# Four of eight cache pieces move from the head of the first tail into the second mixer

## The chip, the cores and the metric

The kernel runs on one core of one Trainium2 chip. The metric is the device time of one launch in microseconds (us), lower is better. A profiled execution of the same program gives the trace; times inside the kernel are counted from the start of its span.

## The reference

Two consecutive layers of a decoder trunk, for 256 prompt tokens and 8 samples of 4 tokens each, all in 32-bit floats. Each layer is a mixer (the second one is dilated sliding-window attention over cached keys and values) followed by a tail. In the tail every token picks its experts by a product-key search and reads one row of `u_tab` and one of `v_tab` for each; this is most of the traffic.

```python
def _tail(x, p, norm_ffn, peer_wq, peer_keys, peer_u, peer_v, norm_ple, ple_gate, ple_proj):
    x = x + _peer(_rmsnorm(x, norm_ffn), peer_wq, peer_keys, peer_u, peer_v).astype(x.dtype)
    gate = jax.nn.sigmoid((_rmsnorm(x, norm_ple) @ ple_gate).astype(jnp.float32))
    ...
def _mixer_dilated_sample(h, pos, caches, w_in, w_out):
    ...
        kv_all = jnp.concatenate([cache, kv_new], axis=1)
        o, l = _dilated_gather_attn(q[:, :, gi], kv_all, L, dil, win // dil)
        outs.append(o)
        lses.append(l)
        keep = min(win, L + T)
        bufs.append(kv_all[:, L + T - keep:])
```

The last line matters here: the key and value caches come back as outputs, so their old rows have to be copied from an input tensor to an output tensor. That copy depends on nothing that is computed.

## The kernel before

**Stages.** The program runs in this order: first norm, first mixer (up to about 239 us), first tail (239 to about 1061 us), second mixer (1061 to about 1503 us), second tail (to the end). They are separated by barriers of all engines.

**A tail.** The engines first do a head: the output projection (line 1818), a norm, the query products (1855), the scores, and on DVE the search that yields the indices of the experts. Then come 288 slots of work. For each, POOL issues an indirect DMA (line 2044) that gathers 128 rows of 8 KB, one for each partition, into one of ten ring buffers (six in `tail_ring`, four in `mid_wring`); DVE takes the dot products (line 1621), ACT makes a diagonal matrix from them (1734 to 1742), and PE adds the weighted rows up (1895). A buffer is reused when PE is done with it. The search for the next 32 slots runs on DVE between the dot products of these.

**The cache copies.** They are HBM to HBM transfers that SP issues. The large ones are cut by `roll_pieces` into pieces of 256 rows, 2.1 MB each (written `32x16384` in the order of instructions, `out_kv_s<-in_cache_kv_w` in the trace). The first mixer copies 32 pieces of the three caches. Of the 32 pieces of the largest cache, which are four for each sample, the first mixer copies the first 8, the head of the first tail copies 8 more (line 2003), and the last `4 * LATE` = 16 are left to the second mixer (line 2679). The second tail copies none; its head is otherwise the same.

**SP's order.** SP issues in program order, and all its DMAs go to one hardware queue, q1 in the trace; those that POOL issues go to q0. In the head of the first tail SP issues the tail's weights and constants (lines 1990 to 2001), then the copies (2003), and after a wait for the projections the rest (2005 and 2009).

**The second mixer.** PE goes through 18 weight chunks of 2 MB (`w_qkv`), numbered c = 0 to 17, in a buffer for two. When chunk c has been multiplied, SP issues the load of chunk c + 2 (line 2687), and right behind it `BESIDE[c]` cache pieces (line 2679), before the stores of the sample rows. Beside the products PE works on side jobs: for chunks 3 to 5 and 12 to 14 the cached keys of the samples, for chunks 6 to 8 and 15 to 17 their values. Keys and values reach it through `mix_ring`, four buffers that POOL fills (line 2710), each when PE has freed it.

**How the pieces are dealt out.** `HEAD[0]` is the number that the first tail's head copies, `LATE` the number of samples that are left to the second mixer, and `BESIDE` says behind which chunk how many go. What `BESIDE` does not name, one piece, is issued before chunk 0. Before, the chunks with pieces are 0, 1, 2, 9, 10, 11 and 17.

Of the kernel before, what the change touches and what calls it, by code (L numbers as in the profile page):

```python
# [2056 lines left out]
UNITS = [(j, it) for it in range(2) for j in range(HH)]  # L2057


LATE = 4  # L2060
HEAD = (8, 0)
EARLY = 0
BESIDE = {0: 2, 1: 2, 2: 2, 9: 2, 10: 2, 11: 2, 17: 3}


def late_pieces(T):

    return roll_pieces(T, 2, range(DEC_B - LATE, DEC_B), 256)


def dilated_phase(nc, K, T, wring, w_in, mixT, w_out_in, late_out):
# [16 lines left out]
    with ExitStack() as ctx:  # L2088
# [60 lines left out]
        with nc.Block() as block:  # L2149
# [487 lines left out]
            def _(sp):  # L2637

                def store(n):
                    c, t = JOBS[n]  # L2640
                    half, kind, g = SECTION(c)
                    o, p = TILES[t]
                    heads = slice(half * HH, half * HH + HH)
                    keep = min(PATTERNS[g][0], SEQ)
                    if kind == 0:
                        return
                    if kind == 1:
                        m = TURNED.index(n)
                        sp.wait_ge(roped, m + 1)
                        src, done = rows[:, m % 4], row_stored[m % 4]  # L2650
                    else:
                        sp.wait_ge(copied, n + 1)
                        src, done = (v[:, t, g] if t < 2 else v_rows[:, g:g + 1]), v_stored
                    if t < 2:
                        if kept(g, t):
                            sp.dma_start(T[f"out_kv{g}_p"][0, 0, o - SEQ + keep:o - SEQ + keep + 128, kind - 1, heads, :],
                                         src).then_inc(done, 16)
                        return
                    full = T[f"out_kv{g}_s"].shape[2]
                    for j in range(HH):  # L2660
                        sp.dma_start(T[f"out_kv{g}_s"][0, :, full - DEC_T:full, kind - 1, half * HH + j, :],
                                     src[32 * j:32 * j + 32, 0, :]).then_inc(done, 16)
                    if kind == 2:
                        if half and g == 0:
                            sp.wait_ge(s_out, 1)
                        for j in range(HH):
                            sp.dma_start(v_new[32 * g:32 * g + 32, j * 128:j * 128 + 128], v_rows[32 * j:32 * j + 32, g, :]
                                         ).then_inc(v_moved, 16)
# [7 lines left out]
                def copies(n):  # L2676
                    for _ in range(n):
                        to, frm = late.pop(0)
                        sp.dma_start(to, frm).then_inc(late_out, 16)

                copies(len(late) - sum(BESIDE.values()))
                for c in range(18):
# [7 lines left out]
                    if c == 17:  # L2690
                        store(3 * c + 2)
                    copies(BESIDE.get(c, 0))
                    if c < 17:
# [28 lines left out]
def build(nc, T):  # L2722

    with ExitStack() as ctx:
# [6 lines left out]

        rolls = [(to, frm, cache_out) for gi, samples, rows in ((1, range(DEC_B), 256), (2, range(DEC_B - LATE), 256),
                                                                (0, range(DEC_B), 128))
                 for to, frm in roll_pieces(T, gi, samples, rows)]
        rolls += [(to, frm, cache_out) for to, frm in late_pieces(T)[:EARLY]]
        with ExitStack() as c2:
            P1 = Phase(nc, c2, "mid")
            wring = P1.sb("wring", [128, 2, KC, 512])
            with ExitStack() as c3:
# [3 lines left out]
                first_norm_phase(nc, K, T, hT, [(wpiece[:, s], T["w_ab"][:, s], w_ab_in[s]) for s in range(4)])  # L2743
                conv_delta_phase(nc, K, T, wring, w_ab_in, w_out_in, mixT, rolls[:24] + rolls[24 + HEAD[0]:])
            w_in, w_out1_in = [P1.sem(f"w_in{i}") for i in range(2)], [P1.sem(f"w_out1_in{i}") for i in range(2)]
            tail_phase(nc, K, T, 0, wring, [(wring[:, c], T["w_qkv"][:, c], w_in[c]) for c in range(2)], w_out_in,
                       rolls[24:24 + HEAD[0]])
            dilated_phase(nc, K, T, wring, w_in, mixT, w_out1_in, late_out)
# [8 lines left out]
def roll_pieces(T, gi, samples, rows):  # L2757

    src, dst = T[f"cache_kv_w{PATTERNS[gi][0]}"][0], T[f"out_kv{gi}_s"][0]
    keep = dst.shape[1] - DEC_T  # L2760
    drop = src.shape[1] - keep
    flat = lambda ap: ap.rearrange("r k h e -> r (k h e)")
    return [(flat(dst[b, r:min(r + rows, keep)]), flat(src[b, drop + r:drop + min(r + rows, keep)]))
            for b in samples for r in range(0, keep, rows)]
# [72 lines left out]
```

## Time and profile before

| | us |
|---|---|
| device time, median of 3 runs | 2307.76 |
| lowest and highest | 2306.37, 2308.43 |
| the profiled execution's device time | 2298.09 |
| its span | 2296.3 |
| busy: PE, DVE, ACT, POOL | 1915.7, 1250.6, 768.8, 701.6 |
| DMA queues q0 and q1, data | 669.72 MB, 203.51 MB |
| mean granted clock of TensorE | 0.946 of full speed |

How to read the rows below. In the page, "GB/s" has one number for each fortieth of the span (57.4 us). A row by windows gives, for a stretch of time, its length, the busy time of PE, weight load, DVE, ACT and POOL with the number of instructions, and then the granted TensorE clock, the DMA share and the GB/s. The DMA share is the time that packets took on the 16 DMA engines, over the stretch; packets are booked whole, so short stretches can read a little over 1. A row of the DMA queues gives packets, MB and share. A row by time gives start, duration, engine, line, operation, tiles, count, and in brackets how long the engine had idled before and what released it. SPq is SP's issuing of a DMA. A copy's bytes are counted once.

### The profile page before, as it was taken

What the parts mean: (1) busy time and instruction counts of PE and PEld (TensorE: products, weight loads), DVE (VectorE), ACT (ScalarE), POOL (GpSimd) and SP (SyncE); (2) the same over time, 40 slices, a digit from 0 to 9 for tenths busy, and PEclk for the clock granted to TensorE, in tenths of its full rate; (3) what the DMA queues carried; (4) which work ended last, traced back from release to release, by engine and by line L of the source; (5) the groups of instructions that cost most, each with busy time, mean ns of one, the idle gap of its engine ahead of it and who ended that gap; (6) DMA issues with size and microseconds to landing.
All of it is one profiled execution on the core that took longest, in us unless ns stands there. A gap on an engine that the chain in (4) does not pass through costs nothing. (4 is left out here: it accounts for less than half of the span.)

```text
span 2296.3 us, 25833 instructions
## 1 busy us (share of the span) xinstructions
PE 1915.7 (83%) x9121; PEld 905.4 (39%) x9121; DVE 1250.6 (54%) x3091; ACT 768.8 (33%) x2251; POOL 701.6 (31%) x709
## 2 busy tenths in 40 slices
PE   7997758878889888767999999889897789888865
PEld 6675424432234322223445644554343223332221
DVE  6974346665675777552110301247755766766654
ACT  2322124433443444342110311215433434433443
POOL 3211124434444533430001010014443344444441
PEclk9998879989999999977999999999998999999977
DMA  9999999999999999997979687949999999999995
GB/s 343 397 348 350 326 369 427 426 428 427 427 427 427 405 427 427 427 428 281 363 296 358 250 328 274 344 190 412 427 427 428 427 427 426 427 427 427 426 427 217
DMA packets 120352, 874.87 MB, mean 381 GB/s; under 512 B 19710, under 2 KB 24830, under 8 KB 34456
## 3 DMA queue, kind: packets, MB, share of 16 engines
q0 software_dynamic: 93328, 669.72, 70.2%
q1 hardware_dynamic: 26896, 203.51, 23.8%
q8 instruction: 72, 1.18, 0.2%
q14 instruction: 56, 0.46, 0.1%
HBM read 861.87 MB, written 118.81 MB: 427 GB/s over the span
## 5 line engine op out<-in xcount | busy, mean ns | idle before, releaser
L1895 PE MATMUL tail_acc<-tail_ring,tail_diag 128*128 128x512 f32 x1248 | 622.6, 628 | 154.8 <-ACT tail_diag L1742 153.5
L1621 DVE CUSTOM_DVE_ANT_0 tail_ring<-tail_ring,all_h 128x1024 f32<-128x1024 f32 x348 | 424.2, 1224 | 293.4 <-DMA tail_ring<-in_peer_uv,tail_idx 291.9
L2044 POOL DMA_INDIRECT tail_ring<-in_peer_uv,tail_idx x348 | 366.9, 1054 | 674.5 <-PE tail_acc L1895 487.7
L1895 PE MATMUL tail_acc<-mid_wring,tail_diag 128*128 128x512 f32 x800 | 391.1, 620 | 72.9 <-ACT tail_diag L1742 72.7
L1895 PEld LDWEIGHTS tail_acc<-tail_ring,tail_diag 128*128 128x128 f32 x1248 | 222.3, 194 | 529.7 <-ACT tail_diag L1742 331.7
L1621 DVE CUSTOM_DVE_ANT_0 mid_wring<-mid_wring,all_h 128x1024 f32<-128x1024 f32 x228 | 278.5, 1224 | 174.3 <-DMA mid_wring<-in_peer_uv,tail_idx 173.6
L1734 ACT ACTIVATE tail_gelus<-tail_dots 128x1 f32<-128x1 f32 x576 | 116.4, 202 | 755.6 <-DVE tail_dots L1621 754.8
L2044 POOL DMA_INDIRECT mid_wring<-in_peer_uv,tail_idx x228 | 250.0, 1097 | 315.4 <-PE tail_acc L1895 264.1
L2166 PE MATMUL mix_acc<-mid_wring,all_hT 128*128 128x512 f32 x576 | 273.8, 610 | 1.5 <-PEq L80 1.4
L1895 PEld LDWEIGHTS tail_acc<-mid_wring,tail_diag 128*128 128x128 f32 x800 | 143.1, 193 | 304.8 <-ACT tail_diag L1742 185.1
L1742 ACT ACTIVATE tail_diag<-all_ident,tail_weights 128x128 f32<-128x128 f32 x512 | 205.5, 401 | 24.2 <-PE tail_acc L1895 7.7
L1739 ACT ACTIVATE tail_weights<-tail_gelus,tail_gate 128x1 f32<-128x1 f32 x576 | 169.8, 295 | 18.7
L2166 PEld LDWEIGHTS mix_acc<-mid_wring,all_hT 128*128 128x128 f32 x576 | 103.3, 193 | 111.7 <-issue 111.1
L2390 DVE TENSOR_TENSOR mix_r<-mix_acc,mix_rope 128x128 f32<-128x128 f32 x24 | 7.0, 292 | 190.1 <-ACT mix_rows L2500 190.1
L420 PE MATMUL mix_banks<-all_hT,mid_wring 128*128 128x288 f32 x384 | 104.3, 423 | 3.7 <-DVEq L1012 2.1
L420 PEld LDWEIGHTS mix_banks<-all_hT,mid_wring 128*128 128x128 f32 x384 | 72.4, 195 | 27.3 <-issue 6.1
L2710 POOL DMA_DIRECT2D mix_ring<-in_kT x32 | 17.0, 534 | 215.0 <-PE mix_wide L2207 178.1
L2417 DVE SCALAR_TENSOR_TENSOR mix_s<-mix_scores_p,mix_band 128x384 f32<-128x384 f32 (+1 forms) x12 | 9.1, 755 | 121.0 <-PE mix_scores_p L2281 120.9
L1818 PE MATMUL tail_acc<-mid_wring,all_mixT 128*128 128x512 f32 x128 | 60.7, 633 | 16.2 <-PEq L80 16.2
L1855 PEld LDWEIGHTS tail_spare<-all_hT,tail_w_big 128*128 128x128 f32 x512 | 67.1, 191 | 15.5 <-issue 15.2
L1855 PE MATMUL tail_spare<-all_hT,tail_w_big 128*128 128x128 f32 (+1 forms) x512 | 68.6, 288 | 2.1 <-ACT all_hT L1707 2.1
L1000 DVE SCALAR_TENSOR_TENSOR all_mixT<-mix_padded_a,mix_taps_a,all_mixT 128x256 f32<-128x256 f32 x120 | 62.3, 548 | 1.2
(472 smaller groups left out, 1755.3 us busy)
## 6 DMA issues: line engine op xcount, KB each, us to landing
mid_wring<-in_w_qkv SPq DMA_DIRECT2D x18, 2048.0 KB, 9.5
mix_ring<-in_kT POOLq DMA_DIRECT2D x16, 1024.0 KB, 10.3
mix_ring<-in_v_rows POOLq DMA_DIRECT2D x16, 1024.0 KB, 10.0
out_kv_s<-in_cache_kv_w SPq DMA_DIRECT2D x8, 2016.0 KB
mid_wring<-in_w_ab SPq DMA_DIRECT2D x12, 1024.0 KB, 11.0
mix_ring<-in_kT POOLq DMA_DIRECT2D x16, 768.0 KB, 10.3
mix_ring<-in_v_rows POOLq DMA_DIRECT2D x16, 768.0 KB, 9.6
tail_w_big<-in_w_query SPq DMA_DIRECT2D x8, 1024.0 KB, 9.3
```

What stands on the lines that cost most here:

```text
L420: last = mm(acc_of(j), wpiece[:, s % 4, k, j % 2 * 128:j % 2 * 128 + 128], hT[:, k, :], start=(k == 0), stop=(k == KC - 1))
L1000: ch.step(STT(out=ca[:, c, 0:SEQ], in0=pa[:, c, k:k + SEQ], scalar=wa[:, c, k:k + 1], in1=ca[:, c, 0:SEQ], op0=ALU.mult, op1=ALU.add))
L1621: V.tensor_tensor_reduce(out=u, in0=u, in1=h[:, g, :], scale=1.0, scalar=0.0, op0=ALU.mult, op1=ALU.add, accum_out=dots[:, n:n + 1]).then_ ...
L1734: ch(A(gelus[:, n:n + 1], dots[:, n:n + 1], ACT.Gelu))
L1739: ch(A(weights[:, n:n + 1], gelus[:, n:n + 1], ACT.Copy, scale=gate[:, j, i:i + 1]))
L1742: A(diag[:, n % DIAGS, 0:w], idn[:, 0:w], ACT.Copy, scale=weights[:, n:n + 1]).then_inc(diag_ready, 1)
L1818: last = mm(acc[g][:, c * 512:(c + 1) * 512], mixT[:, k, g * 128:g * 128 + 128], wring[:, c, k, :], start=(k == 0), stop=(k == KC - 1))
L1855: last = mm(sp2[:, i % 2 * 512:i % 2 * 512 + hi - lo], w_query[:, n, k, :], hT[:, k, lo:hi], start=(k == 0), stop=(k == KC - 1))
L1895: last = mm(acc[g][:, c * 512:(c + 1) * 512], diag[:, n % DIAGS, :], v[:, c * 512:(c + 1) * 512], start=first, stop=final)
L2044: pool.indirect_dma_start(slot(r), None, table, bass.IndirectOffsetOnAxis(ap=idx[:, j, i:i + 1], axis=0)).then_inc(landed[r], 16)
L2166: last = mm(acc_of(n), hT[:, kc, o:o + p], w[:, kc, :], start=(kc == 0), stop=(kc == KC - 1))
L2710: pool.dma_start(ring[:, sl % SLOTS_AHEAD, 0:hi - lo], T[name][half, b, :, lo:hi]).then_inc(landed[sl % SLOTS_AHEAD], 16)
```

## The change

Four of the eight pieces that SP issued at line 2003 go to line 2679: one behind the load that follows chunk 5, one behind that of chunk 6, two behind that of chunk 14. `LATE` = 5 hands the four pieces of one more sample to the second mixer, which now has 20. Nothing else is changed; PE, DVE, ACT and POOL have the same instructions in the same order.

```diff
-LATE = 4
-HEAD = (8, 0)
+LATE = 5
+HEAD = (4, 0)
 EARLY = 0
-BESIDE = {0: 2, 1: 2, 2: 2, 9: 2, 10: 2, 11: 2, 17: 3}
+BESIDE = {0: 2, 1: 2, 2: 2, 5: 1, 6: 1, 9: 2, 10: 2, 11: 2, 14: 2, 17: 3}
```

SP's instructions in the head of the first tail, before (-) and now (+). The first two rows load constants, and the last two are the embedding weights and the sample rows:

```order
 L2000 DMA tail0_gain_b<-in_norm_ple 128x1024
 L2001 DMA tail0_pT<-in_pT0 128x576
-L2003 DMA out_kv2_s<-in_cache_kv_w2048 32x16384 x8
+L2003 DMA out_kv2_s<-in_cache_kv_w2048 32x16384 x4
 L2005 DMA all_mixT<-in_w_emb0 128x2048
 L2009 DMA all_h<-all_hs 32x256 x16
```

Four issues are gone between the constants and the embedding weights.

SP's instructions in the second mixer after chunks 5 and 6 of the first half; `mid_wring<-in_w_qkv` is the load of a weight chunk, `mix1_rows`, `mix1_v` and `all_h` are stored as new cache rows, and `mix1_v_new` is filled for the samples' values:

```order
 L2656 DMA out_kv2_p<-mix1_rows 128x512 x2
 L2687 DMA mid_wring<-in_w_qkv 128x4096
+L2679 DMA out_kv2_s<-in_cache_kv_w2048 32x16384
 L2661 DMA out_kv2_s<-mix1_rows 8x4x128 x4
 L2656 DMA out_kv0_p<-mix1_v 128x512
 L2687 DMA mid_wring<-in_w_qkv 128x4096
+L2679 DMA out_kv2_s<-in_cache_kv_w2048 32x16384
 L2661 DMA out_kv0_s<-all_h 8x4x128 x4
 L2667 DMA mix1_v_new<-all_h 32x128 x4
```

A piece stands behind the weight load of chunk 7 and one behind that of chunk 8, ahead of the small stores.

The same engine after chunk 14, in the second half:

```order
 L2656 DMA out_kv2_p<-mix1_rows 128x512 x2
 L2687 DMA mid_wring<-in_w_qkv 128x4096
+L2679 DMA out_kv2_s<-in_cache_kv_w2048 32x16384 x2
 L2661 DMA out_kv2_s<-mix1_rows 8x4x128 x4
 L2656 DMA out_kv0_p<-mix1_v 128x512
```

Two pieces stand behind the weight load of chunk 16, and the load of chunk 17, issued after the last row shown, comes behind them in the same queue.

## Rows read from the trace of the kernel before

**Rows 1.** The page: the span, and GB/s in 40 equal slices.

```profile
span 2296.3 us, 25833 instructions
...
GB/s 343 397 348 350 326 369 427 426 428 427 427 427 427 405 427 427 427 428 281 363 296 358 250 328 274 344 190 412 427 427 428 427 427 426 427 427 427 426 427 217
```

**Rows 2.** Waits from 345 to 1030 us: engine, releaser, us in total, times, longest.

```profile
DVE tail_ring L1621 <- DMA tail_ring<-in_peer_uv,tail_idx: 126.5, 118, 4.8
```

**Rows 3.** Windows: the first tail's slots, and the head of the second tail.

```profile
340.00:1020.00 680.00, 565.52 (x1480) 223.06 (x1478) 446.28 (x1036) 278.25 (x876) 292.21 (x269) 0.95 1.01 425
...
1522.00:1538.00 16.00, 13.63 (x89) 8.89 (x82) 11.78 (x53) 3.38 (x8) 0.79 (x1) 1.00 0.01 5
```

**Rows 4.** Order of time, first tail: first product, copies, first gather, slots 0 and 20.

```profile
238.95 1.19 PE L1818 MATMUL tail_acc<-mid_wring,all_mixT 128*128 128x512 f32 x1 [14.97 <-PEq L80]
...
245.13 4.99 SPq L2003 DMA_DIRECT2D out_kv_s<-in_cache_kv_w  x8
...
273.22 1.06 POOL L2044 DMA_INDIRECT tail_ring<-in_peer_uv,tail_idx  x1 [50.90 <-DVE tail_top L1562]
...
300.24 1.23 DVE L1621 CUSTOM_DVE_ANT_0 tail_ring<-tail_ring,all_h 128x1024 f32<-128x1024 f32 x1 [18.86 <-DMA tail_ring<-in_peer_uv,tail_idx]
...
367.25 1.23 DVE L1621 CUSTOM_DVE_ANT_0 tail_ring<-tail_ring,all_h 128x1024 f32<-128x1024 f32 x1 [1.20 <-DMA tail_ring<-in_peer_uv,tail_idx]
```

**Rows 5.** The same view of the second tail: first product, and dot product of slot 20.

```profile
1504.03 1.17 PE L1818 MATMUL tail_acc<-mid_wring,all_mixT 128*128 128x512 f32 x1 [1.23 <-PEq L80]
...
1601.38 1.23 DVE L1621 CUSTOM_DVE_ANT_0 tail_ring<-tail_ring,all_h 128x1024 f32<-128x1024 f32 x1 [1.20 <-DMA tail_ring<-in_peer_uv,tail_idx]
```

**Rows 6.** DMA queues from 275 to 310 us: packets, MB, share.

```profile
q1 hardware_dynamic: 242, 10.20, 80.6%
q0 software_dynamic: 221, 1.68, 16.2%
```

**Rows 7.** DMA queues from 1274 to 1300 us: one weight chunk and two pieces.

```profile
q1 hardware_dynamic: 240, 6.29, 64.7%
```

**Rows 8.** SP's weight loads behind chunks 6 and 14, in order of time.

```profile
1203.94 0.35 SPq L2687 DMA_DIRECT2D mid_wring<-in_w_qkv  x1
...
1399.04 1.04 SPq L2687 DMA_DIRECT2D mid_wring<-in_w_qkv  x1
```

**Rows 9.** Windows of the second mixer, around chunks 5 to 8.

```profile
1196.00:1203.00 7.00, 7.00 (x77) 3.37 (x79) 2.53 (x3) 0.95 (x2) 0.00 (x0) 1.00 0.01 2
...
1213.00:1225.00 12.00, 12.00 (x168) 6.46 (x171) 0.00 (x0) 0.60 (x1) 2.65 (x5) 1.00 0.89 315
1225.00:1260.00 35.00, 32.87 (x447) 18.16 (x440) 0.00 (x0) 1.75 (x4) 5.84 (x11) 1.00 1.00 385
```

**Rows 10.** DMA queues from 1204 to 1213 us, in the gap behind chunk 6.

```profile
q1 hardware_dynamic: 556, 2.32, 68.9%
```

**Rows 11.** Windows of the second mixer, around chunks 14 to 17.

```profile
1408.00:1414.00 6.00, 6.00 (x41) 2.40 (x43) 2.53 (x3) 0.00 (x0) 0.00 (x0) 1.00 0.00 0
1414.00:1425.00 11.00, 11.00 (x121) 6.45 (x121) 0.90 (x2) 3.71 (x8) 0.00 (x0) 1.00 0.62 228
1425.00:1460.00 35.00, 32.31 (x412) 16.62 (x411) 0.00 (x0) 1.47 (x3) 6.37 (x12) 1.00 0.95 361
```

**Rows 12.** POOL's key loads, first and twelfth refill, half 0 and half 1.

```profile
1126.62 0.53 POOL L2710 DMA_DIRECT2D mix_ring<-in_kT  x1 [60.31 <-PE mix_wide L2207]
...
1164.84 0.54 POOL L2710 DMA_DIRECT2D mix_ring<-in_kT  x1 [2.17 <-PE mix_wide L2213]
...
1343.04 0.53 POOL L2710 DMA_DIRECT2D mix_ring<-in_kT  x1 [87.61 <-PE mix_wide L2207]
...
1376.81 0.53 POOL L2710 DMA_DIRECT2D mix_ring<-in_kT  x1 [2.17 <-PE mix_wide L2213]
```

**Rows 13.** DMA queues from 1127 to 1131 us, and the window 1134 to 1150 us.

```profile
q1 hardware_dynamic: 20, 1.05, 74.1%
...
1134.00:1150.00 16.00, 12.48 (x68) 4.04 (x56) 0.55 (x4) 0.87 (x2) 1.59 (x3) 0.79 0.99 404
```

## The prediction

> **What bounds the kernel now.** The page comes first: from the seventh slice to the eighteenth, and again from the twenty-eighth on, nearly every slice reads 427 GB/s, and no slice reads more than 428 [rows 1]. These are the two tails. In the slots of the first tail the DMA share is 1.01 for 680 us on end while PE is busy for 565.52 and DVE for 446.28 [rows 3], and DVE's dot products wait for gathers 118 times in `tail_ring` alone [rows 2]. So the first tail is bound by the DMA engines: whatever is taken out of them there shortens it, and a transfer costs nothing only if it lies where they would stand still. The second mixer is the other way round: PE is busy for 32.87 of 35 us, 12 of 12, 7 of 7, while the DMA share goes down to 0.01 and 0.00 in places [rows 9, 11]. A transfer that lies in such a gap is hidden there, one that pushes a ring load back is not.
>
> The kernel as a whole is a chain of stages behind barriers, so the change in time is the sum of what the first tail gives back and what the second mixer takes.
>
> **The price of a piece.** Between 1274 and 1300 us one weight chunk and two pieces pass and nothing else of weight: 6.29 MB in 64.7% of 26 us, that is 16.8 us [rows 7]. A chunk of 2.1 MB at the tail's 427 GB/s [rows 1] is 4.9 us, which leaves 11.9 us for two pieces, 5.95 us each. A piece both reads and writes HBM and moves at about 352 GB/s, slower than a gather. While copies run beside gathers, from 275 to 310 us, q1 spends 80.6% of 35 us on 10.20 MB, or 2.77 us per MB, which is 5.8 us for a piece [rows 6]. I take 5.95. The Trainium skill ("DMA: Bandwidth & Descriptors", Specifications) gives a fabric ceiling of 435 GB/s; by it a piece would take 4.8 us and four 19.3 us. The trace disagrees for copies, at 5.8 to 5.95 us in two places, and it decides.
>
> **Removed: four pieces from the first tail's head.** SP issues the eight from 245.13 us on, the first gather is issued at 273.22 us, and its dot product starts only at 300.24 us, since q1 is full of copies [rows 4, 6]. Would the engines stand still without them? The second tail is the same head with no copies, and it shows it: there the DMA share is 0.01 from 1522 to 1538 us [rows 3], 16 us between the last constants and the first gather. Four pieces of 5.95 us are 23.8 us, more than 16, so the four that stay still fill that hole (the last 7.8 us of them beside the first gathers), and the four that go were all outside it. The gain is 4 x 5.95 = 23.8 us.
>
> A second way to the same number: from the first product of the tail to the dot product of slot 20 the first tail takes 367.25 - 238.95 = 128.30 us [rows 4], the second 1601.38 - 1504.03 = 97.35 [rows 5]. Eight pieces thus cost 30.95 us; the sum from prices gives 8 x 5.95 - 16 = 31.6. With four pieces it is 7.8, so 30.95 - 7.8 = 23.1 us come back. The lower bound is four pieces at a weight chunk's speed, 4 x 4.9 = 19.6 us. The upper bound adds what the gathers lose beside copies: 1.68 MB in 16.2% of 35 us, 5.7 us, where 427 GB/s would take 3.9 [rows 6], so 1.8 us more, 25.6. I take 23.8. What is late next in the head are DVE and PE, which finish search and queries before the first slot; the second tail, where they are all that is waited for, still reaches slot 20 in 97.35 us [rows 5], so they bar nothing. Behind the copies in q1 stand the embedding weights and the sample rows, wanted many slots later; they come earlier. SP's four issues less cost or save nothing.
>
> **Added: one piece behind chunk 5.** It follows a weight load in q1 and starts when that has landed. From 1196 to 1203 us the DMA share is 0.01 [rows 9], 7 us of hole for 5.95 us of piece. No ring load is issued until 1213. Cost 0. Behind it in q1 are stores that nobody waits for soon.
>
> **Added: one piece behind chunk 6.** The weight load is issued at 1203.94 us [rows 8]. From 1204 to 1213 us q1 is busy for 68.9% of 9 us [rows 10], so 2.8 us are free, of which I count 2.0, since part of it lies ahead of the load's first packets. The following 12 us have a share of 0.89, 1.3 us free, and then 35 us follow with 1.00 [rows 9], where PE already idles for 35 - 32.87 = 2.1 us. So 5.95 - 2.0 - 1.3 = 2.65 us are pushed into a stretch that is full and whose value loads PE waits for. That is one bound. The other is a row of the same kind: behind chunk 2 two pieces end some 4 to 5 us after POOL's first key refill at 1126.62; from 1127 to 1131 us only q1 moves, 20 packets for 1.05 MB [rows 13], and no ring load. Twelve refills take 1164.84 - 1126.62 = 38.22 us there, and in the second half, where the pieces are through before the first refill, 1376.81 - 1343.04 = 33.77 [rows 12]. That collision costs 4.45 us, clock included: the granted clock is 0.79 from 1134 to 1150 us, where PE idled [rows 13]. Here the piece would end near 1217, about 4 us after the first value refill at 1213. I take 3.0 us, nearer to the work that is pushed, because 1.3 us of it are absorbed; both ends stay in the range. The Trainium skill ("DMA: Bandwidth & Descriptors", Queues, rings and completion order) says that a DMA engine goes round the queues a packet at a time. Rows 6 agree in kind: beside large copy packets q0 had 16.2% of the time. By it the ring load is held up for as long as the piece lasts, which is the 4.45 us end.
>
> **Added: two pieces behind chunk 14.** The load is issued at 1399.04 us [rows 8]. Free are 6.0 us from 1408 to 1414 and 38% of 11 us, 4.2, up to 1425, in all 10.2 for 11.9 us of pieces; the remaining 1.7 us fall into 35 us with a share of 0.95, which has 1.75 us free [rows 11]. The load of chunk 17 comes behind the pieces, some 4 us late, and is wanted a whole chunk later. The large copy packets are over by about 1420, before the value refills of this half begin at about 1425. Cost 0 to 1.7, and 4.45 if it collides after all; I take 0.5.
>
> **The sum.** -23.8 + 0 + 3.0 + 0.5 = -20.3 us. The trace is one execution with a span of 2296.3 us and a device time of 2298.09; the median of the runs is 2307.76, 0.4% above. The change is taken off that median: 2287.5 us.
>
> **The rivals.** *The mixer hides everything.* For it speaks that three of the four pieces have a hole of their own. It gives 2307.8 - 23.8 = 2284, or 2282 with the mixing loss. Against it stands the collision behind chunk 2. *The head gives back only half.* If PE or DVE in the first 30 slots became what is waited for, as after a long idle with the clock down, some 12 us of the gain would be left: 2307.8 - 12 + 3.5 = 2299. The 97.35 us of the second tail speak against it. *The time only moves.* If every piece takes its 5.95 us from PE in the mixer, 23.8 us are paid for 23.8: about 2308, no change. It would need holes of 7 and 6 us to be unusable. *Slower: starved ring loads.* Pieces keep whole ring loads and the load of chunk 17 back, PE stands and its clock drops to 1.2 GHz after each stall. PE then pays 4 x 5.95 = 23.8 and for each of the two places what the slow clock costs, at 0.79 for 16 us some 3.4 us: 30.6 against 23.8, so 2315. This decides from where the mixer loses more than 23.8 us; the nearest row is 4.45 for one collision, five times less.
>
> **How the numbers follow.** The forecast, a head gain of 20 to 26 and a mixer cost of 1 to 8, gets 0.74; the mixer that hides everything 0.10; half the gain 0.08; no change 0.04; slower 0.04. A measurement of this kernel tells about 0.2%, 4.6 us, from no change, so faster is 0.74 + 0.10 + 0.08 = 0.92. The range: at the low end 2307.8 - 25.6 = 2282, less the runs' spread of some 2 us, 2280; at the high end a gain of 19.6 against two collisions of 4.45, 10.7 us net, 2297, and 1 for the spread, 2298.
>
> **What the profile after would show.** Right: the dot product of slot 0 starts around 285 us instead of 300.24; slot 20 comes 104 to 105 us after the first product instead of 128.30, and the DMA share stays near 1 between 250 and 340 us. The first tail ends 23 to 24 us earlier. In the second mixer the holes before chunk 7's end and behind chunk 14 fill up, the twelve value refills from about 1213 (24 us earlier in the new count) take up to 4.5 us longer, and the chunks 15 to 17 keep their pace. Wrong: a hole in the head's DMA share, which would mean that four pieces don't reach the first gather; PE waiting for a weight chunk anywhere in the mixer; or new waits for value loads after chunk 14.

## The result

| | before | after |
|---|---|---|
| device time, median | 2306.37 us (2303.95 to 2308.43) | 2281.77 us (2279.84 to 2284.59) |
| ratio | | 0.9893, 95% interval 0.9882 to 0.9905 |
| span of the profiled execution | 2296.3 us | 2278.0 us |

The kernel is 24.6 us faster. The forecast was 20.3 us less, with 2280 to 2298 as its range. In a later series of runs the same two kernels gave 2306.96 and 2281.86 us, ratio 0.9888, interval 0.9871 to 0.9905.

### The profile page after: what moved, and what is told of

The parts are those of the page before. It is cut to its first block and busy times, and to the rows that moved or that the text cites. A ratio compares the mean times of both kernels' runs of the same rounds, so it can differ in the third digit from the quotient of the medians.

```text
span 2278.0 us, 25833 instructions
## 1 busy us (share of the span) xinstructions
PE 1923.2 (84%) x9121; PEld 913.4 (40%) x9121; DVE 1250.0 (55%) x3091; ACT 769.1 (34%) x2251; POOL 697.6 (31%) x709
```

## The profile after

The page of the changed kernel, in the lines that answer to [rows 1] and to the small table: the span, GB/s in 40 equal slices, and the two queues with packets, MB and share.

```profile
span 2278.0 us, 25833 instructions
...
GB/s 335 396 346 351 311 407 427 427 428 427 426 427 425 415 427 427 427 366 309 376 332 348 222 394 336 297 233 412 427 427 428 426 427 426 427 427 426 427 427 217
...
q0 software_dynamic: 93328, 669.72, 70.6%
q1 hardware_dynamic: 26896, 203.51, 24.1%
```

The packets and bytes of both queues are those of before. The sixth slice, 369 before, is now 407: the DMA engines come to pure gathers sooner.

The changed kernel in order of time, the rows that answer to [rows 4]: first product of the first tail, and the dot products of slots 0 and 20.

```profile
241.81 1.19 PE L1818 MATMUL tail_acc<-mid_wring,all_mixT 128*128 128x512 f32 x1 [9.62 <-PEq L80]
...
290.10 1.23 DVE L1621 CUSTOM_DVE_ANT_0 tail_ring<-tail_ring,all_h 128x1024 f32<-128x1024 f32 x1 [6.32 <-DMA tail_ring<-in_peer_uv,tail_idx]
...
345.41 1.23 DVE L1621 CUSTOM_DVE_ANT_0 tail_ring<-tail_ring,all_h 128x1024 f32<-128x1024 f32 x1 [1.20 <-DMA tail_ring<-in_peer_uv,tail_idx]
```

Slot 0 comes 48.29 us after the first product (61.29 before), slot 20 after 103.60 us (128.30 before). Windows of the same kernel, columns as in [rows 3]: the head up to the first gathers, and the slots.

```profile
248.00:283.00 35.00, 32.63 (x170) 17.49 (x169) 20.97 (x87) 4.22 (x12) 5.86 (x6) 1.00 1.05 387
...
343.00:1000.00 657.00, 539.38 (x1400) 210.42 (x1399) 427.90 (x990) 265.52 (x839) 276.01 (x259) 0.96 1.01 426
```

No hole opens before the first gather, which is issued at 275.61 us. Behind it there is a short dip: from 283 to 285 us the share is 0.34, some 1.3 us of idle time. The slots run at the same 1.01 as before. So the stage was cut short at its front and nowhere else.

Three windows of the second mixer after the change, for [rows 9] (time 21.4 us earlier): ahead of chunk 6's weight load, the 9 us behind it, and the 35 us of value loads.

```profile
1174.59:1181.59 7.00, 7.00 (x74) 3.31 (x76) 2.53 (x3) 0.89 (x2) 0.00 (x0) 1.00 0.39 162
1182.59:1191.59 9.00, 9.00 (x57) 4.65 (x58) 0.91 (x2) 3.11 (x7) 0.00 (x0) 1.00 1.09 420
...
1203.59:1238.59 35.00, 32.89 (x445) 17.90 (x434) 0.00 (x0) 1.75 (x4) 5.83 (x12) 0.95 0.98 377
```

Both holes take up work: in the first, 0.01 became 0.39, and the gap behind chunk 6 is full. PE's busy time in the 35 us is 32.89 us against 32.87, at a granted clock of 0.95 against 1.00.

Cut into stages, the two traces give:

| stage | before, us | after, us |
|---|---|---|
| first product of the first tail | 238.95 | 241.81 |
| from there to the start of the second mixer | 822.59 | 797.93 |
| second mixer | 442.45 | 445.69 |
| second tail | 792.31 | 792.57 |

The head gave back 24.7 us. The sum of the rows is only 18.3 us, against 24.6 for the medians, because the first and third rows rose by 2.9 and 3.2. Whether the change did that is what the first experiments had to tell. It also matters which execution was traced: that of before took 2298.09 us, 8.3 us less than the median, that of the changed kernel 2279.84 us, 1.9 us less.

## Experiments

**The kernel before, once more.** No edit.

> The kernel before, unchanged, for a second trace and to see what a comparison of equal kernels shows. Ratio 1.000 within 0.002. In the two traces so far the change of span (-18.3 us) is smaller than that of the medians (-24.6 us); 2.9 us of this are a later first product of the tail (241.81 against 238.95 us), where the granted clock was 0.50 instead of 1.00 for some 15 us. If that is chance, the first product moves by a few us here too, while first product to slot 20 stays at 128.3 us and the second mixer at 442.5 us, each within 1 us. If instead the piece moved changed the first mixer, it stands at 238.95 again.

Measured: 2307.71 us against 2307.04, ratio 1.000 (0.9989 to 1.0011). First product at 240.25 us, slot 20 after 129.19, tail to mixer 824.94, second mixer 444.30. The mixer was thus 1.8 us longer than in the other trace of the same program, a little more than the 1 us that I had allowed. The excess of the third row is partly chance; the next runs say how much.

**The head's part alone.** Four pieces are copied nowhere.

```diff
-LATE = 4
-HEAD = (8, 0)
+LATE = 5
+HEAD = (4, 0)
 def late_pieces(T):
-    return roll_pieces(T, 2, range(DEC_B - LATE, DEC_B), 256)
+    return roll_pieces(T, 2, range(DEC_B - 4, DEC_B), 256)
```

> The head's part of the change alone: the first tail copies four pieces, the second mixer its 16 as before, and the other four pieces are copied nowhere (one sample's old rows are missing from the output). Theory (a piece outside the hole costs 5.95 us of DMA time, and the mixer takes a little): first product to slot 20 about 103.6 us as after the change, second mixer 442.5 us as before, so 24 to 27 us less than before, and 2 to 3.5 us less than the change. Rival (the mixer hides all four, and what its stage gained in length is chance): no more than 1 us less than the change, with a mixer of 445 us sometimes.

Measured: 2282.14 us, ratio 0.9891 (0.9873 to 0.9908), the change's own ratio. Slot 20 after 103.84 us, and the second mixer took 450.7 us with no piece added to it, longer than with the four pieces in the trace of the change. The theory's 2 to 3.5 us for the mixer are not seen; the rival, that the mixer hides all four, fits better. It is not shown by the time alone: the two ratios are 0.0002 apart (0.5 us), and each is known to 3 or 4 us only.

**Only two pieces in the head, and none.** The same edit with six and with all eight pieces left out.

```diff
-HEAD = (4, 0)
+HEAD = (2, 0)
...
-                conv_delta_phase(nc, K, T, wring, w_ab_in, w_out_in, mixT, rolls[:24] + rolls[24 + HEAD[0]:])
+                conv_delta_phase(nc, K, T, wring, w_ab_in, w_out_in, mixT, rolls[:24] + rolls[28:])
```

> The first tail copies only two pieces, six are left out altogether, the second mixer copies 16 as before. Theory with the hole of 16 us between the last constants and the first gather: two pieces are 11.9 us and fit in, so first product to slot 20 is 97.4 us, 30.9 us less than before. Rival without a hole (every piece costs its 5.95 us wherever it is in the head): 6 x 5.95 = 35.7 us less, slot 20 at 92.6 us.

> No cache copies in the first tail at all, eight pieces left out, the second mixer as before. Theory: the hole is empty and nothing more is gained, slot 20 at 97.4 us as with two pieces, 30.9 us less than before. Rival: 8 x 5.95 = 47.6 us less. A third possibility, that large packets disturb gathers well beyond their own time, would show as a few us between this kernel and that with two pieces.

Measured: with two pieces 2276.15 us (ratio 0.9872, 0.985 to 0.9894), 30.9 us less than before, slot 20 after 98.18 us. With none 2272.89 us (0.986, 0.9841 to 0.9879), slot 20 after 98.15 us. The linear rivals wanted 92.6 us for slot 20, and 47.6 us less in time with none. Windows of the kernel with none: weights and constants, then the hole up to the packets of the first gather, which is issued at 274.95 us.

```profile
241.00:257.00 16.00, 15.90 (x32) 6.94 (x32) 0.69 (x1) 0.00 (x0) 0.00 (x0) 0.85 0.92 338
257.00:274.00 17.00, 14.63 (x127) 9.56 (x126) 12.14 (x47) 3.46 (x8) 0.00 (x0) 1.00 0.17 67
274.00:276.00 2.00, 2.00 (x6) 0.92 (x5) 1.97 (x13) 0.00 (x0) 1.04 (x1) 1.00 0.00 0
276.00:278.00 2.00, 2.00 (x7) 0.93 (x6) 1.97 (x12) 0.45 (x2) 1.39 (x3) 1.00 0.66 164
```

There is the hole: 17 us with a DMA share of 0.17, 2 us with 0.00 and 2 us with 0.66 leave 14.1 + 2.0 + 0.7 = 16.8 us in which the engines stood still. The first two pieces in it cost slot 20 nothing (98.15 and 98.18), the next two 5.4 us, the last four 24.7. The 3.3 us between the two medians don't show at slot 20, and their intervals overlap. From the first product to the second mixer the traces have 794.55 us with two pieces and 791.98 with none, so 2.6 us lie behind slot 20; two traces of one kernel differ by as much there (822.59 and 824.94), and what they are is not settled.

**Four pieces behind chunk 6, then two.** The head and the number of pieces as in the change.

```diff
-BESIDE = {0: 2, 1: 2, 2: 2, 5: 1, 6: 1, 9: 2, 10: 2, 11: 2, 14: 2, 17: 3}
+BESIDE = {0: 2, 1: 2, 2: 2, 6: 4, 9: 2, 10: 2, 11: 2, 17: 3}
```

> All four moved pieces stand behind chunk 6 (one behind 5 and two behind 14 are moved there), the head with four as in the change. Theory (pieces that still run when the value refills begin keep them back, and the work that finds no hole is paid by PE): of 23.8 us of pieces 2.0 and 1.3 us find room, the load of chunk 9 comes behind them too, so the step from chunk 7's weight load to chunk 8's grows from about 29 us (27.2 to 30.2 in five traces without a piece there) by some 15 to 20 us, the granted clock drops while PE stands, and the kernel is 12 to 20 us slower than the change. Rival (the ring and the load's early issue hide pieces here too, as they seem to hide the one piece of the change): under 5 us slower.

Measured: 2297.9 us, ratio 0.9978 (0.9966 to 0.999), so most of the gain is gone, some 20 us. From the weight load behind chunk 6 to the one behind chunk 7, which below is called the step from chunk 6's weight load to chunk 7's, it takes 38.46 us instead of 21.96. In the kernel with four pieces behind chunk 6, the queues from 1198 to 1219 us, where the value refills are in flight, and PE's wait for them (us in total, times, longest):

```profile
q1 hardware_dynamic: 145, 6.36, 83.3%
```

```profile
PE mix_wide L2244 <- DMA mix_ring<-in_v_rows: 17.5, 3, 15.0
```

This is the slower rival's mechanism, in the open: 15.0 us of one wait while q1 holds the engines.

```diff
-BESIDE = {0: 2, 1: 2, 2: 2, 5: 1, 6: 1, 9: 2, 10: 2, 11: 2, 14: 2, 17: 3}
+BESIDE = {0: 2, 1: 2, 2: 2, 6: 2, 9: 2, 10: 2, 11: 2, 14: 2, 17: 3}
```

> Two pieces behind chunk 6, the one behind chunk 5 moved there; the rest as in the change. With four pieces behind chunk 6 the two steps after it, from chunk 6's weight load to chunk 8's, took 66.1 us; in ten traces with none they took 49.2 to 52.2, mean 50.8. So 23.8 us of pieces cost 15.3, and 8.5 us were hidden. If there is such an allowance of 8.5 us behind chunk 6 (holes, and what is loaded ahead in the ring), one piece of 5.95 costs nothing and two cost 11.9 - 8.5 = 3.4 us: 54.2 us for the two steps. Rival (each piece costs a quarter of the four, 3.8 us): 58.4 us, and the one piece of the change should have cost 3.8. The time is 2 to 8 us over that of the change, which is hard to tell; the steps decide.

Measured: the two steps took 26.95 + 27.72 = 54.67 us, against 54.2 from the allowance and 58.4 from the rival; the time was 2287.38 us (0.991, 0.9886 to 0.9935), some 4 to 5 us above the change by the ratios. Steps from chunk 6's weight load to chunk 8's by the number of pieces behind chunk 6: none 50.8 us (ten traces, 49.2 to 52.2), one 50.8 and 50.4, two 54.7, four 66.1. PE's wait for value loads in the kernel with two:

```profile
PE mix_wide L2244 <- DMA mix_ring<-in_v_rows: 6.0, 3, 3.4
```

and in the changed kernel, with one:

```profile
PE mix_wide L2244 <- DMA mix_ring<-in_v_rows: 2.1, 1, 2.1
```

Before, with none, it also was 2.1 us in total, and 2.6 in the second trace of that kernel. The second trace of the change has 3.3 us, and the kernel that leaves four pieces out, with none behind chunk 6, 3.8. One piece there makes no wait that stands out of this spread.

**The piece behind chunk 6 moved to chunk 10, beside the change.**

```diff
-BESIDE = {0: 2, 1: 2, 2: 2, 5: 1, 6: 1, 9: 2, 10: 2, 11: 2, 14: 2, 17: 3}
+BESIDE = {0: 2, 1: 2, 2: 2, 5: 1, 9: 2, 10: 3, 11: 2, 14: 2, 17: 3}
```

> The change with the one piece behind chunk 6 put behind chunk 10 instead, where the trace has a hole of 10 us after the two pieces. Theory: the same time as the change within 0.1%, the step from chunk 7's weight load to chunk 8's within the 27.2 to 30.2 us of the other traces. Rival, the forecast's own term for this piece: 3.0 us faster than the change.

> The changed kernel as it is, for a second trace and to stand beside the next two on one chip. Ratio to before 0.989 to 0.991. Theory (the mixer hides the one piece behind chunk 6; the 3.2 us by which the stage was longer in the first trace are its ordinary spread): first product to slot 20 at 103 to 104 us, second mixer between 442 and 451 us as in the traces without the pieces, with no new steps. Rival (the piece costs 3 us): never below 445.5 us.

Measured in one series: the change 2281.86 us (0.9888), the variant 2284.38 us (0.9904, 0.9889 to 0.992). Taking the piece away from chunk 6 gained nothing; the 2.5 us on the other side are 0.11%, a little over what was expected, and the ratios' intervals overlap. The second mixer took 450.26 us in this trace of the change, inside 442 to 451. But the rival's mark, never below 445.5 us, is met too, by 450.26 and by 445.69 in the first trace: the length of the mixer does not decide between them. The steps and the moved piece do.

**Shorter descriptors in the head.** The kernel before, with each head piece issued as two half-width copies.

```diff
-                    sp.dma_start(to, frm).then_inc(done, 16)
+                    for c in range(2):
+                        sp.dma_start(to[:, c * 1024:c * 1024 + 1024], frm[:, c * 1024:c * 1024 + 1024]).then_inc(done, 16)
```

> The kernel before with its eight head pieces each issued as two half-width copies, so that a descriptor is 4 KB long instead of 64 KB; same bytes, same place. Theory of the packet round (a gather packet waits behind one large copy packet each turn): the first gather lands much earlier, slot 0 starts 42 to 50 us after the first product instead of 61.3, but the DMA time of the bytes is the same, so slot 20 stays at 128 us or a little more and the time within 0.2% of before. Rival (order of issue decides, gathers wait for q1 to drain): slot 0 stays at 61 us. If the loss of gathers beside large packets, 1.8 us, is real, slot 20 comes about that much earlier, unless short descriptors cost more.

Measured: 2301.43 us against 2301.74, ratio 0.9996 (0.9979 to 1.0013). Slot 0 after 44.09 us instead of 61.29. The queues of this kernel from 280 to 350 us:

```profile
q0 software_dynamic: 2644, 19.30, 65.6%
q1 hardware_dynamic: 2646, 10.24, 35.7%
```

The two queues moved nearly the same number of packets, 2644 and 2646, which fits taking turns one for one, so the share of a queue follows the size of its packets. With large ones q1 took 80.6% and the gathers 16.2% [rows 6], here it is the other way round, and the time stays the same. Slot 20 came after 121.19 us, 7 us sooner than I wrote. It starts at 361.10 us; the copies run up to about 355 us, and the small loads behind them in q1 up to about 376. Part of q1's work is thus still to come at slot 20, which in this kernel is no measure of the whole. To the start of the second mixer it took 820.71 us against 822.59 and 824.94 before, 2 to 4 us less. That is the size of the mixing loss, but also near the spread.

**Filling the holes.** A version built on these readings: one more sample's pieces go to the second mixer and to the hole of the second tail's head, and what the first tail's head copies is four pieces of 1 MB.

```diff
-LATE = 5
+LATE = 6
 HEAD = (4, 0)
-BESIDE = {0: 2, 1: 2, 2: 2, 5: 1, 6: 1, 9: 2, 10: 2, 11: 2, 14: 2, 17: 3}
+BESIDE = {0: 2, 1: 2, 2: 2, 5: 1, 9: 3, 10: 3, 11: 2, 14: 2, 17: 4}
+CLOSE = 2
...
-            tail_phase(nc, K, T, 1, wring, (), w_out1_in)
+            tail_phase(nc, K, T, 1, wring, (), w_out1_in,
+                       [(to, frm, late_out) for to, frm in late_pieces(T)[-CLOSE:]])
```

> A version meant to beat the change. One more sample's pieces leave the first mixer and the head: the head copies four small pieces of 1 MB (12 us, which fit the hole of 16), the first mixer 28 copies instead of 32 (four small ones less), the second mixer 22 pieces (three behind chunks 9 and 10, four behind 17, none behind 6), and the head of the second tail two, in its own hole of 16 us. Theory: slot 20 at 98 us instead of 103.6 (5.6 us less), the second mixer unchanged at 442 to 451 us, the second tail's slot 20 unchanged at 95 to 97 us, the first product of the first tail up to 5 us earlier: 5 to 10 us faster than the change, 2272 to 2277. Rival (the second mixer has no more free holes): the mixer or the second tail grow by 6 us or more and the time stays at 2281.

> The version with the head down to 4 MB of small pieces, 22 pieces in the second mixer and two in the second tail's head, again, on one chip with the change. Theory: 5.7 us from slot 20 (97.9 against 103.6 us) and nothing paid elsewhere, so 4 to 8 us faster than the change. If the 13 us that the two ratios of different chips suggest (0.9837 against 0.9893) are real, something else is gained too, and it has to show as an earlier first product or a shorter second mixer.

Measured: 2263.06 us against 2301.74 in one series of runs, ratio 0.9837 (0.9815 to 0.9859), and 2270.62 against 2306.96 in another, 0.985 (0.983 to 0.9871). Beside the change in that series it is 11.2 us faster, more than the 4 to 8 of my sum. Slot 20 comes after 97.92 and 97.12 us, and in the second tail after 95.79 and 95.87, so its two pieces are hidden; the second mixer took 444.30 and 451.58 us. The second trace shows one more thing. Its first product of the first tail:

```profile
230.17 1.19 PE L1818 MATMUL tail_acc<-mid_wring,all_mixT 128*128 128x512 f32 x1 [6.81 <-PEq L80]
```

In the first trace of the same kernel it is:

```profile
245.64 1.19 PE L1818 MATMUL tail_acc<-mid_wring,all_mixT 128*128 128x512 f32 x1 [3.89 <-PEq L80]
```

The granted clock from 200 to 205 us is 1.00 in the trace that ends the stage at 230 us and 0.50 in the other. In all others the first product lies between 238.95 and 245.58 us. The earliest, the trace of before, had a clock of 1.00 there too and still got only to 238.95, with 32 copies in the first mixer instead of 28. Four more traces with 32 copies had 1.00 there and their first product at 240.25 to 241.89 us; in the second trace of before, PE was busy for none of the last 15 us, from 225 to 240, at a DMA share of 0.60. So with 32 copies a held clock alone did not end the stage sooner. That fewer copies let it end sooner when the clock holds is likely, but rests on one trace: two traces of one kernel differ by more than any effect looked for.

To tell it apart, the first mixer with 24 copies, and 8 MB of small pieces in the head:

```diff
-HEAD = (4, 0)
+HEAD = (8, 0)
```

> The same, but the head copies all eight small pieces (8.1 MB, as many bytes as the four large ones of the change) and the first mixer only 24. Theory: slot 20 at 103.6 us as in the change; anything gained comes from the first mixer, whose DMA share is near 1 for most of 200 us. If the first mixer is bound by DMA, the first product comes up to 23 us earlier than at 240 to 242 us and this beats the other version; if its copies are hidden behind PE, the first product moves by less than 3 us and this kernel is 5 us slower than the other version, about like the change.

Measured: 2268.5 us, ratio 0.985 (0.9828 to 0.9872), slot 20 after 102.21 us, first product at 240.96 us. It is 5.4 us behind the other version in the same series, of which the fuller head explains 4.3 (slot 20), and its first product is no earlier than elsewhere. So in this trace, with a granted clock of 0.50 from 200 to 225 us, the first mixer wasn't bound by its DMA traffic: the share was down to 0.10 from 205 to 225 us, while PE was busy for all 20. But I had expected a time about like the change's, and by the two ratios, taken in different series, it is some 10 us below. Its trace shows no stage that is shorter by as much. The traced executions were not the typical ones, though: 2274.64 us here, 6.1 above the median, and 2276.46 us in the first trace of the other version, 13.4 above it and the slowest of five. Of those five, the three at 2259.49 to 2263.06 us had a mean granted clock of 0.951 to 0.953, the two at 2273.32 and 2276.46 one of 0.943 and 0.945. An earlier end of the first mixer in the executions whose clock holds would fit all of this; no trace of the fastest ones exists, and it stays open.

## Why the prediction was right, and where it was off

**What bounds the first tail.** Right. The stage lost what was taken out of its DMA queue, and its slots went on at a share of 1.01.

**The price of a piece.** Slightly low. From first product to the second mixer the kernels with eight head pieces took 822.59 and 824.94 us, those with four 797.75 to 799.43 (six traces), so four pieces are worth 25.3 us, 6.3 each, where the sum had 23.8. The upper bound of 25.6, with the loss of gathers beside large packets, was nearer the truth. Pricing the four at the fabric ceiling of 435 GB/s that the Trainium skill gives ("DMA: Bandwidth & Descriptors", Specifications), an estimate of 19.3 us, comes out 6 us too low here.

**The marks in the trace.** Slot 20 came 103.6 us after the first product, where 104 to 105 were forecast, slot 0 after 48.3 where 46 were. The stage ended 24.7 us earlier in the first pair of traces, counted from its first product, where 23 to 24 were forecast, and no hole opened before the first gather.

**The hole of 16 us.** Right, and shown by taking pieces out: 98.2, 98.2, 103.6 and 128.3 us to slot 20 with none, two, four and eight. Without copies the engines stand still for 16.8 us. At 5.95 us a piece, four hide 23.8 - 5.4 = 18.4 us by slot 20, and eight 47.6 - 30.1 = 17.5. The comparison with the second tail, which has no copies, had found it in the trace of before.

**The piece behind chunk 5** cost nothing, as said. **The two behind chunk 14:** 0.5 us forecast. The step from chunk 15's weight load to chunk 16's takes 21.96 us in every trace. The next, to chunk 17's, takes 26.6 to 29.1 us without them and 26.7 to 29.4 with them (means of seven traces each 27.4 and 28.3), so a price of 0.5 us is below what these traces can tell.

**The piece behind chunk 6.** Wrong in size: 3.0 us forecast, with 2.65 as the low bound, and nothing was paid. The step that failed is the one that let everything beyond the holes of 2.0 and 1.3 us be paid by PE. Four pieces there cost 15.3 us of their 23.8 and two cost 3.9 of 11.9, so 8 to 8.5 us are hidden, not 3.3. What hides them beyond the idle DMA time is argued, not shown: PE enters the stretch with four value buffers already loaded (POOL issued these at 1146.10 to 1154.80 us and the next at 1191.81). The 35 us that I took as full, share 1.00, read 0.98 with the piece in front, so nothing more was pushed into them. The bound from the key loads, 4.45 us, was the price of something else: there two pieces stand behind one chunk, 11.9 us, and an allowance of some 8, if it holds there too, leaves about 4. Counted by pieces it agrees with the 3.9 of two behind chunk 6.

**The sum.** -20.3 forecast, -24.6 and -25.1 measured: 1.5 us from the price of the pieces, and up to 3.5 from the mixer, whose steps show no cost. The rival "the mixer hides everything", at 2282 to 2284 with a chance of 0.10, was the case that came true. That a single pair of traces said 18.3 is chance, most of it in the trace of before, 8.3 us under its median: over the traces the first product moved between 238.95 and 245.58 us in all kernels but the last version, and a mixer without the extra pieces between 440.95 and 450.7.

**The slower rival** is real where pieces are piled up: four behind one chunk take 16.5 us in one step.

## What to carry to other kernels

In a stage that is bound by its DMA engines, a background copy costs its full engine time, except where the engines would stand still: find that hole by a sister stage that lacks the copy, and leave just as much in it as it holds. Behind a weight load of a stage that PE bounds, more can be hidden than the idle DMA time; load such a place in steps, and the cost starts at a point (here 8 us against 3.3 us of idle time) rather than at zero. Take the length of a stage from several traces before a difference of 3 us is explained, and look how far the traced execution lies from the median.

## What was not expected of the hardware

Two busy queues moved nearly equal numbers of packets (2644 and 2646), so a queue of 4 KB copies left 65.6% of the time to 8 KB gathers, and one of large packets 16.2%; the total didn't change. One program's granted clock can fall at the same place in one execution and not in the next: from 200 to 205 us it was 0.50 in a trace whose first tail began at 245.64 us, and 1.00 in another of the same kernel, where it began at 230.17. With 32 copies in the first mixer the stage hardly followed it: 238.95 to 241.89 us with 1.00, 241.10 to 242.48 with 0.50.
